# Moving work between TensorE, VectorE and the row gathers in a hymba + PEER block: gate product first, sums a round later, ten rows earlier, identity turns

## The reference, cut to what matters

```python
mod = (c @ w_mod[l] + b_mod[l])[:, None, :]          # 6 x 1024, c is one vector
shift1, scale1, gate1, shift2, scale2, gate2 = jnp.split(mod, N_MOD, axis=-1)
h = rmsnorm(x, g_pre_mix[l]) * (1.0 + scale1) + shift1
aq, ak, av, mq, mk, mv, mi, mf, mo = jnp.split(h @ w_in[l], IN_SPLITS, axis=-1)
att = sliding_window_attention(rope(aq), rope(ak), av, att_sinks[l])
mh = mlstm_chunkwise(*silu(conv(mq, mk)), mv, mi + b_igate[l], mf + b_fgate[l])
mh = rmsnorm(mh, mlstm_norm_g[l]) * jax.nn.sigmoid(mo)
x = x + gate1 * rmsnorm(jnp.concatenate([att, mh], axis=-1) @ w_out[l], g_post_mix[l])
h2 = rmsnorm(x, g_pre_ffn[l]) * (1.0 + scale2) + shift2
# peer_ffn: per token and head, top 16 of 128 on each half of the query, top 16 of the
# 256 sums -> 128 experts a token; y = sum_k gelu(u[e_k] . h2) * gate_k * v[e_k]
x = x + gate2 * rmsnorm(peer_ffn(h2, ...), g_post_ffn[l])
```

## Time and profile before

| | |
|---|---|
| median of 3 runs | 1596.32 us (1591.72 to 1598.09) |
| the profiled execution, whole | 1594.46 us |
| its span in the trace | 1592.5 us |
| mean granted clock of TensorE | 0.983 |
| PE busy | 1520.5 us (95%) |
| DVE busy | 1390.9 us (87%) |
| ACT busy | 605.5 us (38%) |
| POOL busy | 501.6 us (31%) |
| HBM read, written | 421.63 MB, 32.25 MB |

### The profile page before, as it was taken

One profiled execution on the slowest core, in us unless ns is written; L12 is line 12 of the kernel. 1 busy time (PEld: TensorE's weight loads), 2 busy tenths in 40 slices (PEclk: granted clock), 3 DMA queues, 4 the chain that ended last, 5 costly groups with the idle time before them and its releaser, 6 DMA issues.

```text
span 1592.5 us, 23089 instructions
## 1 busy us (share of the span) xinstructions
PE 1520.5 (95%) x8322; PEld 1284.3 (81%) x8322; DVE 1390.9 (87%) x2974; ACT 605.5 (38%) x976; POOL 501.6 (31%) x424
## 2 busy tenths in 40 slices
PE   3998999799999999999899999999999999999997
PEld 2454654488899999999898999999999989787885
DVE  5885896679999768999598999999999999999997
ACT  2101441522355565544233333333333333443443
POOL 1000000033010200033355555555555555343430
PEclk8999999899999999999999999999999999999999
DMA  9663250132264657798999999999999999999993
GB/s 349 230 213 135 86 212 1 39 97 104 75 227 143 229 169 221 247 300 297 413 380 410 391 409 408 391 405 395 408 406 394 406 397 373 377 389 402 395 392 134
DMA packets 175737, 455.70 MB, mean 286 GB/s; under 512 B 14924, under 2 KB 73412, under 8 KB 173448
## 3 DMA queue, kind: packets, MB, share of 16 engines
q1 hardware_dynamic: 108224, 229.74, 39.8%
q0 software_dynamic: 58176, 211.87, 34.4%
q10 hardware_dynamic: 9224, 12.62, 2.3%
HBM read 421.63 MB, written 32.25 MB: 285 GB/s over the span
## 4 chain that ended last, share of the span: by engine, by line
PE 64%; DVE 6%; DMA 1%; ACT 1%; issue 1%; DVEq 0%; ACTq 0%
PE peer_psum L1595 17%; PE peer_psum L1599 9%; PE peer_psum L1655 7%; PE peer_psum L1662 7%; PE peer_psum L1670 7%; PE peer_psum L1642 4%; PE peer_psum L1659 3%; PE peer_psum L1665 3%; PE peer_psum L1607 3%; PE peer_psum L1580 3%; DVE s_all L1777 2%; PE peer_psum L1588 1%; DVE s_all L1773 1%; DMA s_all<-in_peer_v 1%; DVE hT L1737 1%
## 5 line engine op out<-in xcount | busy, mean ns | idle before, releaser
L1595 PE MATMUL peer_psum<-hH,hi_slots 128*128 128x320 f32 x1024 | 308.8, 315 | 5.6 <-DVE lo_slots L1888 2.4
L1595 PE MATMUL peer_psum<-hL,hi_slots 128*128 128x320 f32 x1024 | 303.5, 310 | 0.0
L1466 POOL DMA_INDIRECT hT<-in_peer_u,eidx x128 | 150.7, 1177 | 309.3 <-DVE dots L1737 268.4
L1502 ACT ACTIVATE hi_slots<-s_all 128x1024 fp32r<-128x1024 f32 x128 | 135.9, 1062 | 189.7 <-PE peer_psum L1670 183.5
L1466 POOL DMA_INDIRECT hT<-in_peer_v,eidx x128 | 151.1, 1180 | 175.3 <-DVE s_all L1746 162.6
L1595 PEld LDWEIGHTS peer_psum<-hH,hi_slots 128*128 128x128 f32 x1024 | 193.8, 189 | 10.2 <-issue 4.8
L1595 PEld LDWEIGHTS peer_psum<-hL,hi_slots 128*128 128x128 f32 x1024 | 193.9, 189 | 2.9
L1599 PE MATMUL peer_psum<-hH,lo_slots 128*128 128x320 f32 x1024 | 171.7, 310 | 0.0
L1874 DVE TENSOR_TENSOR lo_slots<-s_all,hi_slots 128x1024 fp32r<-128x1024 f32 x128 | 156.0, 1219 | 14.7 <-ACT hi_slots L1502 14.4
L1746 DVE SCALAR_TENSOR_TENSOR s_all<-hT,coef,s_all 128x1024 f32<-128x1024 f32 x126 | 161.0, 1278 | 3.0 <-DMA hT<-in_peer_v,eidx 2.6
L1599 PEld LDWEIGHTS peer_psum<-hH,lo_slots 128*128 128x128 f32 x1024 | 157.9, 189 | 3.4
(11 more groups left out here) (309 smaller groups left out, 2904.4 us busy)
## 6 DMA issues: line engine op xcount, KB each, us to landing
ring<-in_peer_u SPq DMA_DIRECT2D x128, 512.0 KB, 7.4
s_all<-in_peer_v SPq DMA_DIRECT2D x128, 512.0 KB, 7.0
gate_table<-lot SPq DMA_DIRECT2D x16, 1280.0 KB, 6.5
lot<-gate_table SPq DMA_DIRECT2D x16, 1280.0 KB, 11.0
lot<-in_w_mod SPq DMA_DIRECT2D x5, 2048.0 KB, 11.6
x_sb<-in_w_mod POOLq DMA_DIRECT2D x10, 1024.0 KB, 6.6
gelu_table<-s_all ACTq DMA_DIRECT2D x56, 160.0 KB, 3.3
s_in<-gelu_table SPq DMA_DIRECT2D x56, 160.0 KB, 8.0
```

Source lines behind the costliest of these rows:

```text
L1466: pool.indirect_dma_start(rows_of(j), None, A[table][0], bass.IndirectOffsetOnAxis(eidx[:, k:k + 1], 0)).then_inc(rows_in[j % RG], 16)
L1502: func(H[:, slot_of(w), :], vb[:, w % RING, :], ACT.Copy).then_inc(v_hi, 1)
L1595: mm(ps[:, bank, 0:TD], H[:, b, c * P:(c + 1) * P], h[:, c, T0:T], start=(c == 0 and h is hH), stop=False)
```

## The change

Five edits.

1. **Identity turns.** A new helper `turn_ident(n, name)` has PE transpose the identity matrix n times into a bank that is about to be used and whose content is not read: 36 after the columns of scale1's first half, 14 after those of shift1's first half, 14 ahead of the second half of the "mq" products, 24 ahead of `h2_T(3)`, 12 at the start of `query(0)`.
2. **Output-gate product.** `wide_product("mo", C_MO, 0)` stands ahead of `att_scores(0)` instead of behind `mlstm_scores(0)`; ACT's `out_gate(0)` is its first step of the rounds.
3. **Sums.** Sum 9 leaves the place ahead of `att_soft(1)`. Rounds 1 and 2 make sums 9 and 10 instead of 10 and 11, and sum 11 stands behind the heads' norm, ahead of the norms of the output tiles.
4. **Shift2 and gate2.** The columns of shift2 are made and emptied behind round 2, where gate2's rows were; gate2's rows are made behind `h2_T(0)` and emptied ahead of the norm of output tile 3.
5. **Rows.** `ROWS_LEAD` goes from (14, 20) to (24, 10). Turns 14 to 39 get 24 rows in place of 14 (one each in all turns but 14 and 27), turns 40 to 51 get 10 in place of 20 (before 1, 2, 2, four times; after 0, 1, 1, 1, 1, 1, twice). The 34 together, and all later rows, stay.

```diff
--- before.py
+++ after.py
@@ -70,7 +70,7 @@
 G_END = LEAD - 6
 LESS = 40
 DVE_BEHIND = 11.0
-ROWS_LEAD, ROWS_TAIL = (14, 20), 68
+ROWS_LEAD, ROWS_TAIL = (24, 10), 68
 NF = NBLK - LEAD
 END = LEAD + 2 + NBLK
 ORDER = list(range(LEAD, NBLK)) + list(range(LEAD))
@@ -217,15 +217,15 @@
         order += [("aq", t) for t in range(NT)] + modg(GATE1) + [("kv", t) for t in range(NT)]
         order += [("mv", 0), ("mv", 1), ("gi",), ("gf",), ("mv", 2), ("mv", 3)] + [("modc", SCALE2, h) for h in range(2)]
         order += [("qT", t) for t in range(NT)] + [("kT",), ("gcol",)]
-        order += scores(0) + mscore(0) + [("mo", 0)] + scores(1) + [("modc", SHIFT2, h) for h in range(2)] + [("mo", 1)]
+        order += [("mo", 0)] + scores(0) + mscore(0) + scores(1) + [("mo", 1)]
         order += probsT(0) + mvalue(0) + mscore(1) + av_of(0) + [("mo", 2)]
         order += scores(2) + probsT(1) + mvalue(1) + mscore(2) + av_of(1) + [("mo", 3)]
-        order += scores(3) + probsT(2) + mvalue(2) + mscore(3) + av_of(2) + modg(GATE2)
+        order += scores(3) + probsT(2) + mvalue(2) + mscore(3) + av_of(2) + [("modc", SHIFT2, h) for h in range(2)]
         order += probsT(3) + mvalue(3) + av_of(3)
         out_of = lambda t: [("out", h, t) for h in range(2)]
         h2T_of = lambda t: [("h2T", t, i) for i in range(2)]
         order += out_of(0) + out_of(1) + [("mixT", c) for c in range(4, 8)]
-        order += out_of(2) + h2T_of(0) + out_of(3) + h2T_of(1) + h2T_of(2)
+        order += out_of(2) + h2T_of(0) + modg(GATE2) + out_of(3) + h2T_of(1) + h2T_of(2)
         order += [("keys", i) for i in range(4)] + [("h", i) for i in range(4)] + h2T_of(3)
 
         last_use = {("in", C_MQ): ("mq", 3), ("in", C_AQ): ("aq", 3), ("in", C_AK): ("kv", 3),
@@ -422,6 +422,12 @@
                     last = tr(bk("xT", c)[:, t * P:(t + 1) * P], both[:, t, c * P:(c + 1) * P], ident[:])
                 bk.done(last, "xT", c)
 
+            def turn_ident(n, *name):
+
+                bk.wait_free(pe, *name)
+                for _ in range(n):
+                    tr(bk(*name)[:, 0:P], ident[:], ident[:])
+
             def mod_columns(s, h):
 
                 bk.wait_free(pe, "modc", s, h)
@@ -440,7 +446,9 @@
 
             pe.wait_ge(S["consts"], CONSTS)
             mod_columns(SCALE1, 0)
+            turn_ident(36, "modc", SHIFT1, 0)
             mod_columns(SHIFT1, 0)
+            turn_ident(14, "mq", 0)
 
             w = slab_of(("in", C_MQ))
             wait_slab(pe, ("in", C_MQ))
@@ -450,6 +458,7 @@
                     pe.wait_ge(S["mq_late_in"], 16)
                     mod_columns(SCALE1, 1)
                     mod_columns(SHIFT1, 1)
+                    turn_ident(14, "aq", 0)
                 pe.wait_ge(S["hT_ready"], 4 * half + 4)
                 for j in range(4):
                     if half == 0:
@@ -577,12 +586,10 @@
                                       v_ext[:, s, h, :], start=(s == 0), stop=(s == t))
                     bk.done(last, "mv2", h, i)
 
+            wide_product("mo", C_MO, 0)
             att_scores(0)
             mlstm_scores(0)
-            wide_product("mo", C_MO, 0)
             att_scores(1)
-            for h in range(2):
-                mod_columns(SHIFT2, h)
             wide_product("mo", C_MO, 1)
             att_turn(0)
             mlstm_values(0)
@@ -600,7 +607,8 @@
             mlstm_values(2)
             mlstm_scores(3)
             att_values(2)
-            mod_rows(GATE2)
+            for h in range(2):
+                mod_columns(SHIFT2, h)
             att_turn(3)
             mlstm_values(3)
             def mix_T(c):
@@ -648,6 +656,7 @@
                 out_product(t, range(4, DC))
             out_product(2, range(DC))
             h2_T(0)
+            mod_rows(GATE2)
             out_product(3, range(DC))
             for t in range(1, 3):
                 h2_T(t)
@@ -664,6 +673,7 @@
                     for k in range(4):
                         last = tr(bk("h", 2 * t + i)[0:n, k * P:(k + 1) * P], hT[:, 4 * i + k, t * P:t * P + n], ident[:])
                     bk.done(last, "h", 2 * t + i)
+            turn_ident(24, "h2T", 3, 0)
             h2_T(3)
 
         @block.scalar
@@ -758,9 +768,9 @@
                 bk.wait_full(act, "mo", t)
                 bk.release(func(o_gate[:, t, :], bk("mo", t), ACT.Copy), "mo", t)
 
+            out_gate(0)
             decays(0, range(NT))
             att_exp(0)
-            out_gate(0)
             att_exp(1)
             out_gate(1)
             probs_T(0)
@@ -1089,22 +1099,19 @@
             mod_sum_of(8)
             att_soft(0)
             mlstm_weights(0)
-            mod_sum_of(9)
             att_soft(1)
-            for h in range(2):
-                mod_col(SHIFT2, h)
             att_norm(0)
             for n in range(3):
                 if n:
-                    mod_sum_of(9 + n)
+                    mod_sum_of(8 + n)
                     att_soft(n + 1)
                 probs_T(n)
                 mlstm_out(n)
                 mlstm_weights(n + 1)
                 att_norm(n + 1)
                 att_turned(v.tensor_copy, dve, n, 1)
-            dve.wait_ge(S["g_post2_in"], 16)
-            mod_row(GATE2, gg2, g_post)
+            for h in range(2):
+                mod_col(SHIFT2, h)
             probs_T(3)
             mlstm_out(3)
 
@@ -1120,7 +1127,11 @@
             dve.wait_ge(S["o_gate_done"], 1)
             v.tensor_tensor(wide, wide, o_gate[:], ALU.mult).then_inc(S["mh_done"], 1)
 
+            mod_sum_of(11)
             for t in range(NT):
+                if t == 3:
+                    dve.wait_ge(S["g_post2_in"], 16)
+                    mod_row(GATE2, gg2, g_post)
                 dve.wait_ge(S["mix_sq"], 2 * t + 2)
 
                 step(v.tensor_tensor(stat[:, 0, 8 + t:9 + t], stat[:, 0, 2 * t:2 * t + 1], stat[:, 0, 2 * t + 1:2 * t + 2], ALU.add))
@@ -1267,8 +1278,11 @@
 
             def query(m):
                 s = m // 2
+                bk.wait_free(pe, "q", m)
+                if m == 0:
+                    for _ in range(12):
+                        nc.tensor.transpose(bk("q", m)[:, 0:P], keep["ident"][:], keep["ident"][:])
                 wait_wq_hi(pe, s)
-                bk.wait_free(pe, "q", m)
                 at = slice((m % 2) * P, (m % 2) * P + P)
                 for c in range(DC):
                     if m == 0:
```

## The result

The changed kernel takes 1579.7 us (median of 4 runs, 1576.8 to 1581.2) against 1596.7 (1591.7 to 1598.1): ratio 0.9896, 95% interval 0.9875 to 0.9918. That is 17.0 us less, where 23 were forecast. Measured again for experiment 5, it was 1577.7 against 1595.8, ratio 0.9891 (0.9875 to 0.9907), 18.1 us less. So it is faster, and inside the range of 1566 to 1585; the gain in the forecast's own sum, 22.2, is 5 us too large.

What follows compares the result with a forecast made beforehand. PE (95% busy) and DVE (87%) were taken to be late in turn. −6.7 − 9.3 + 1.7 − 1.0 − 5.6 − 1.3 = −22.2 us gave 1572.3, or 1574.1 by the median, stated as 1573; range 1566 to 1585.

Steps and rivals of the forecast that it cites:

- The head: First products of the mixer: identity turns hold PE's clock at full, saving 0.8, 3.1 and 2.9 us, sum −6.7.
- The fourth sum: DVE's sum at the head ends at 46.8, PE reaches its columns at 46.3 but takes 0.9 first: just not late.
- Round 0: First attention round: gate product first and sum 9 gone let PE and DVE meet at 168.1, not 177.7: −9.3 us.
- The later rounds keep their contents.: Rounds 1 and 2 keep one sum each, shift2's columns (1.84) replace gate2's rows (1.88): no change in time.
- What moved comes back: Behind the rounds: sum 11 and gate2's DVE work hide in idle, gate2's rows on PE cost +1.7 us.
- Query: Query 0's products: identity turns give full clock, but low weights come from DVE at 315.5, so −1.0 us.
- Ten rows: Lead turns 40 to 50: nine rows fewer there, DVE no longer the bound, −5.6 us; free in turns 14 to 39.
- Behind the lead: Up to 790 us, two fewer gathers in the full-DMA stretch: −1.3 us, between 0 and 2.6.
- Rival 1: Head and query: identity turns don't hold the clock; gain only 11.9 us, 1582.6; chance 15%.
- rival 2: Lead: gathers or ACT hold the turns, or DMA behind stays full; gain 15.3, about 1579; chance 14%.
- rival 3: Round 0 not shortened because ACT's exponentials or PE's scores become the wait; gain 12.9, 1581.6; chance 7%.
- rival 4: Lead, behind the last choice: eight rows with six buffers starve, delaying `settle` and one-hot tiles; slower, 1604; chance 2%.

Runs made afterwards that it cites:

- experiment 5: The changed kernel once more, unchanged: 1577.7 us, ratio 0.9891 to the kernel before.
- experiment 2: Changed kernel plus eleven identity turns ahead of the turn of tile 3's probabilities in round 3: 1574.0 us, ratio 0.9858 to the kernel before.
- experiment 1: Changed kernel with all five calls of identity turns left out: 1582.5 us, ratio 0.9908 to the kernel before.
- experiment 7: Changed kernel plus eleven identity turns in round 3 and the first six row gathers spread: 1574.8 us, ratio 0.9851 to the kernel before.
- experiment 9: Changed kernel with tile 0's output-gate product and its emptying back behind the scores, sums, shift2 and gate2 still moved: 1586.1 us, ratio 0.9944.
- experiment 8: Changed kernel with sum 9, shift2 and gate2 back in their old places, output-gate product still early: 1583.7 us, ratio 0.9924.
- experiment 6: Changed kernel with POOL's first six row gathers issued two lead turns apart: 1576.5 us, ratio 0.9872 to the kernel before.
- experiment 3: Changed kernel with `ROWS_LEAD` back at (14, 20): 1584.4 us, ratio 0.9920 to the kernel before.
- experiment 4: Changed kernel with the mixer's old order (gate product, sums, shift2, gate2), identity turns and moved rows kept: 1584.6 us, ratio 0.9924.

## Why the prediction was right, and where it was off

**The head** (−6.7): −6.7 and −6.6 in the two profiles, by the step named, the clock held by transposes. The rule in the prediction, that transposes don't hold the clock, is refuted for this kernel at two places: the head, and round 3 in experiment 2. Three things were too simple. What the low clock costs before the change isn't 6.7 us in each execution (experiment 1). The fourth sum, forecast as just not late, was late for PE in two of the ten profiles with these turns (experiments 7 and 9): PE waited 0.9 us for it, the clock fell to half, the 14 turns themselves took 3.23 and 2.83 us instead of 1.73, and the second slab came 1.8 us later. And the falls further on were not the same when the head ended earlier, which the forecast did not look at.

**Round 0** (−9.3): −10.0 in both. PE and DVE met at 161.0, and ACT gave nothing back. The forecast had this as the sum of two paths, which experiments 8 and 9 bear out: with either path left as it was, 0 and 3.5 us. What it lacked is why PE's path needs edit 4 too.

**"The later rounds keep their contents."** This step failed. They keep their work (columns 1.84 us for rows 1.88), not their clock: from the turn of tile 0's probabilities to the first output product it takes 57.2 us in the first profile and 55.8 in the second, where it took 54.2, so 3.0 and 1.6 were lost. The forecast priced the columns' place by duration and didn't ask what the clock does in a stretch with a wait of 1.20 and narrow work ahead.

**What moved comes back** (+1.7): +1.7, sum 11 and gate2's emptying hidden in DVE's idle as said, though that idle shrank by 4.4 us ahead of tile 0's norm, not by 6. **Query** (−1.0): −0.9 in both, from 8.34 us between the first and the second query to 7.48 and 7.46.

**Ten rows** (−5.6): −5.6 in both, and DVE is no longer the bound. **Behind the lead** (−1.3): from turn 51 to the end −0.9 and −1.3. It is within the scatter of the body, so the reason given (two gathers fewer) is not shown.

**Not in the forecast:** the stall behind the first six gathers, 4.6 and 4.4 us in turns 7 and 8. It goes when the gathers are spread (experiment 6), it comes with the old rows and with the old order too (experiments 3 and 4), and in the kernel before at 0 and 1.6 us. The ten profiles that have the burst sort by where it meets PE's turn. In six POOL issues the first gather 1.3 us ahead of turn 7's first product, and PE loses 3.9 to 4.6. In three, the two of the kernel before and experiment 1, it is 2.8 us ahead, and PE loses 0, 1.6 and 1.7. In the changed kernel's first it is 4.2 us ahead, and PE loses 4.6 at another step of ACT. These groups are also those whose clock has no fall, one of 3.4 and one of 6.8 us at the start of the lead, which delays PE's turns against DVE's choice and so against the gathers. So a part of what a high clock at the start of the lead brings was lost again in the stall. That the place in the turn is the cause is argued from these traces; nobody moved the burst alone by a us or two. The forecast took the rows' gathers for bandwidth only, and looked at the ten that moved and not at the first six.

The clock in round 3 (3.0 and 1.6) and the stall (4.6 and 4.4) are what the sum missed, and the clock at the start of the lead, where the first profile lost 1.4 more than before and the second 1.4 less (its turn 0 ran at full clock throughout). Smaller misses are round 0 (0.7 better), the way from the last output product to the second query (0.2 worse), the head of the second profile (0.1 worse) and what follows turn 51 in the first (0.4 worse). So −22.2 + 3.0 + 4.6 + 1.4 − 0.7 + 0.2 + 0.4 is −13.3, as the first span shows, and −22.2 + 1.6 + 4.4 − 1.4 − 0.7 + 0.2 + 0.1 is −18.0, as the second shows. That the total stayed in the range is in part luck: these two losses, 6 to 8 us together, are in none of its rivals. Rival 1 (turns don't hold) is refuted, rival 2 (lead gives back) and rival 3 (round 0 not shortened) didn't happen, and rival 4's wait came, but below the point where it costs. DVE's waits behind the last choice in the changed kernel:

```profile
DVE more_rows L1751 <- DMA more_rows<-in_peer_u,eidx: 3.8, 1, 3.8
DVE tsum L1767 <- ACT top L1530: 2.3, 1, 2.3
```

Of the eight rows there the seventh waits 0.8 us for its gather and the eighth 3.8, and 2.3 are left of the 8.9 that `settle` waited. By that, an estimate from these waits, hardly another row would have been free there.

## What to carry to other kernels

Where two engines are late in turn, find each engine's path to the same point with the other's wait taken out, and whatever is queued between; moving one side alone may bring nothing. PE's idle gaps cost twice here, once as a wait and once as clock on the products behind them, and dummy transposes in the gap are a cheap cure; but profile more than one execution, and look for what the earlier arrival meets further on (a fall of the clock, a burst of transfers). Gains of a few us ahead of a long body are best read at marks in the trace, since the body's own scatter is as large.

## What the runs showed of the hardware

Transposes of the identity keep TensorE's clock at 2.4 GHz where it is already there: 36 in 4.13 us at the head, 11 in 1.40 in round 3 at a granted 1.00. Where the clock fell in or just behind a wait of 0.9 us ahead of them (experiments 7 and 9, at 49 us), 14 of them took 2.8 to 3.2 us, mostly at half clock, and it was back 3.4 us after it fell. The falls come at gaps but not at the same gap in each execution: round 3 had one of 6.8 or 3.4 us with the same instructions, and none in experiment 1, which had them 4.3 us later.

With six indirect gathers of 512 KB issued within 8 us, ACT stood idle for 4.2 to 6.0 us ahead of one step in nine of the ten profiles that have the burst (1.8 or 0.5 ahead of that step in an ordinary turn), at a loss to PE of 1.6 to 4.6. The profile names "remote" or "issue" as what ACT waited for, and PE's part had been done for 2.8 to 4.3 us in all nine. ACT starts again 8.6 to 8.8 us after the first gather began on POOL (7.9 in experiment 2), whatever its place in the turn. DVE too shows waits for "issue" of 0.4 to 1.0 us there. That the engines' instructions come late through the same DMA engines would fit, and was not tested apart from spreading the gathers.
